# A mixture-of-experts stage: one expert group on all tokens, three groups on gathered tokens

## The reference

```python
p_group = softmax(t @ w_rg + b_rg)
g_val, g_idx = top_k(p_group, 1)
fine_sel = take_along_axis(fine, g_idx[:, :, None], axis=1)[:, 0]
e_val, e_idx = top_k(softmax(fine_sel), 2)
...
for e in range(16):
    y_e = (silu(t @ w1[e]) * (t @ w3[e])) @ w2[e]
    out = out + combine[:, e:e + 1] * y_e
```

## Time and profile before

| | |
|---|---|
| median of three runs | 2156.91 us |
| the profiled execution | 2160.48 us |
| its span (first to last instruction) | 2158.6 us |
| mean granted TensorE clock | 0.919 |
| TensorE, VectorE, ScalarE busy | 87%, 55%, 39% |
| the router's 64 matmuls | 1587.8 to 1601.6 us |
| experts, first to last matmul | 1608.3 to 2153.4 us |

### The profile page before, as it was taken

How to read it: one execution, slowest core, us unless ns; L and a number is a source line. 1 busy time by engine, 2 the same in 40 slices (tenths; PEclk the granted TensorE clock), 3 DMA queues, 4 the chain that set the end, 5 groups by cost and what they waited for, 6 DMA issues and landing times.

```text
span 2158.6 us, 28995 instructions
## 1 busy us (share of the span) xinstructions
PE 1884.3 (87%) x10182; PEld 1542.8 (71%) x10182; DVE 1194.5 (55%) x1894; ACT 844.8 (39%) x1321; POOL 16.1 (1%) x31
## 2 busy tenths in 40 slices
PE   4989887689999995996599978888779999999999
PEld 2833344568888874774489967666569999999998
DVE  3335444354444446788766665664645565555654
ACT  4122221432233234676444543442424444444432
POOL 1000000000000000000000000000000000000000
PEclk9979888879999997998889988898879999999999
DMA  7334563212333330332336633231316665656663
GB/s 279 94 125 156 201 223 122 78 43 95 98 96 97 97 97 11 87 99 77 117 118 193 186 126 98 78 98 59 91 47 185 185 194 175 194 175 193 189 182 117
DMA packets 306495, 279.37 MB, mean 129 GB/s; under 512 B 18954, under 2 KB 248828, under 8 KB 300284
## 3 DMA queue, kind: packets, MB, share of 16 engines
q1 hardware_dynamic: 304752, 269.93, 39.8%
q0 software_dynamic: 1152, 8.39, 1.0%
q10 hardware_dynamic: 524, 0.19, 0.0%
HBM read 277.40 MB, written 1.05 MB: 129 GB/s over the span
## 4 chain that ended last, share of the span: by engine, by line
PE 76%; DVE 13%; ACT 4%; DMA 4%; issue 2%; ACTq 0%; SPq 0%; DVEq 0%; POOL 0%; POOLq 0%
PE bank L366 64%; DMA ada_rows_in<-in_ada_w_dram 3%; PE bank L471 2%; PE bank L858 2%; PE bank L883 2%; PE bank L876 1%; DVE weights_lo L339 1%; PE bank L1163 1%; DVE work L549 1%; DVE x_and_ctx L552 1%; DMA work<-in_c_ctx_dram 1%; PE bank L1213 1%; DVE work L1752 1%; DVE work L1789 1%; DVE act_lo L418 1%
## 5 line engine op out<-in xcount | busy, mean ns | idle before, releaser
L339 DVE TENSOR_TENSOR weights_lo<-stage,weights_hi 128x1024 fp32r<-128x1024 f32 x428 | 516.7, 1220 | 117.2 <-ACT weights_hi L327 114.6
L366 PE MATMUL bank<-act_hi,weights_hi 128*128 128x256 f32 (+1 forms) x1744 | 534.8, 307 | 23.7 <-DVE x_and_ctx L1752 12.4
L366 PE MATMUL bank<-act_lo,weights_hi 128*128 128x256 f32 (+1 forms) x1744 | 533.7, 306 | 0.0
L366 PE MATMUL bank<-act_hi,weights_lo 128*128 128x256 f32 (+1 forms) x1744 | 533.6, 306 | 0.0
L327 ACT ACTIVATE weights_hi<-stage 128x1024 fp32r<-128x1024 f32 x428 | 439.5, 1052 | 155.5 <-PE bank L366 71.7
L366 PEld LDWEIGHTS bank<-act_hi,weights_hi 128*128 128x128 f32 x1744 | 337.8, 194 | 39.3 <-issue 18.2
L366 PEld LDWEIGHTS bank<-act_lo,weights_hi 128*128 128x128 f32 x1744 | 337.7, 194 | 14.3
L366 PEld LDWEIGHTS bank<-act_hi,weights_lo 128*128 128x128 f32 x1744 | 337.4, 193 | 13.4
L366 PE MATMUL bank<-weights_hi,ff_hi 128*128 128x512 f32 x656 | 255.7, 390 | 1.9 <-DVE ff_lo L1916 1.9
L366 PE MATMUL bank<-weights_hi,ff_lo 128*128 128x512 f32 x656 | 255.6, 390 | 0.0
L366 PE MATMUL bank<-weights_lo,ff_hi 128*128 128x512 f32 x656 | 255.4, 389 | 0.0
(11 more groups left out here) (284 smaller groups left out, 1990.2 us busy)
## 6 DMA issues: line engine op xcount, KB each, us to landing
stage<-in_w_dram SPq DMA_DIRECT2D x384, 256.0 KB, 3.3
stage<-in_mlp_w_dram SPq DMA_DIRECT2D x256, 256.0 KB, 3.0
ada_rows_in<-in_ada_w_dram SPq DMA_DIRECT2D x40, 1024.0 KB, 5.0
stage<-in_w_in_dram SPq DMA_DIRECT2D x64, 256.0 KB, 3.2
stage<-in_lru_w_in_dram SPq DMA_DIRECT2D x40, 256.0 KB, 3.5
ada_rows_in<-in_ada_w_dram POOLq DMA_DIRECT2D x8, 1024.0 KB, 13.6
stage<-in_attn_w_qkv_dram SPq DMA_DIRECT2D x24, 256.0 KB, 4.3
stage<-in_lru_w_out_dram SPq DMA_DIRECT2D x20, 256.0 KB, 3.4
```

Of the source, the lines that this page charges most:

```text
L339: dve.eng.tensor_tensor(wlo[u % NRING][:], stage[u % NSTAGE][:], whi[u % NRING][:].bitcast(F32), ALU.subtract).then_inc(sem("lo_ready"), 1)
L366: m = pe.eng.matmul(ps, l, r, start=start and j == 0, stop=stop and j == 2, skip_group_check=True)
```

## The change

- All experts of one group, the one chosen by more than 128 tokens, or else group 0, are computed on all tokens as before (e = 0 to 3 of the new loop). The other three groups are computed on blocks of 128 slots, into which the tokens of that group are gathered (e = 4 to 15).
- To do so, the router's choice of both token tiles is worked out in one pass. TensorE counts tokens by group with a triangular matrix; VectorE derives the wide group, the order of the groups (`order`, four integers) and each token's slot, and writes a 0/1 matrix `SEL` of 256 tokens by 384 slots. TensorE gathers by multiplying the normalized rows (in hi and lo parts) with `SEL`, turns `SEL` for the way back, and brings the combine weights to the slots.
- SyncE waits for `expert_order`, loads four registers from it, and addresses expert weights by register. No expert weight is loaded or split before that (`CAP`). The order of units is w1 of e, w3 of e, w2 of e - 1, and all have 512 columns. The loop over experts is unrolled.
- For a gathered expert tokens are stationary and 512 columns of weights move, so Silu and product lie token by slot; the product is turned by four transposes. The four experts of a group add up in two banks, which are split into hi and lo and scattered back by matmuls with the turned `SEL`.
- The result is stored in four transfers. The semaphores of the norms and residuals are shared between stages. Scratch for the router lies elsewhere.

```diff
+            sp.eng.wait_ge(sem("expert_order"), 1)
+            first = [sp.eng.value_load(order[0:1, g:g + 1], min_val=0, max_val=12) for g in range(4)]
+            def matrix(w, e):
+                return w[0].rearrange("e k n -> k e n")[:, ds(first[e // 4] + e % 4, 1), :].rearrange("k e n -> k (e n)")
...
+            for e in range(NEXP):
+                up_units(w1_2, e)
+                up_units(w3_2, e)
+                if e:
+                    down_units(e - 1)
+            down_units(NEXP - 1)
...
+            t.wait_ge(sem("select"), 2)
+            t.wait_ge(sem("xn_lo"), 2)
+            for d in range(KT):
+                if plan.uses[4 + d % 4]:
+                    t.wait_ge(*pe.bank_free(4 + d % 4))
+                ps = pe.take(("gather", d), 4 + d % 4)
+                for tt in TWO:
+                    for j, src in enumerate((XNH, XNL)):
+                        mm = t.matmul(ps[:, 0:384], src[:, tt, d * P:d * P + P], SEL[:, tt, :],
+                                      start=tt == 0 and j == 0, stop=tt == 1 and j == 1)
+                mm.then_inc(*pe.fill(("gather", d)))
...
+            def expert_up(e, j):
+                if e < 4:
...
+                                mm = three(pe, psum[2 * j + m // 2][:, (m % 2) * TX:(m % 2) * TX + TX],
+                                           wh[:, kk, m * P:m * P + P], wl[:, kk, m * P:m * P + P], hh_(k), hl_(k),
+                                           k == 0 and m % 2 == 0, k == KT - 1, True)
...
+                for kq in range(4):
+                    wh, wl = unit_begin(pe, (2, 512))
+                    for kk in range(2):
+                        k = 2 * kq + kk
+                        mm = three(pe, ps[:], wh[:, kk, :], wl[:, kk, :], gh[:, k, at], gl[:, k, at], k == 0,
+                                   k == KT - 1, False)
+                    unit_end(pe, mm, ("h", e, j) if kq == 3 else None)
...
+            for e in range(NEXP):          # TensorE
+                expert_up(e, 0)
+                if e > 4:
+                    expert_turn(e - 1)
+                expert_up(e, 1)
+                if ends_block(e - 2):
+                    scatter(block_of(e - 2))
+                if e:
+                    expert_down(e - 1)
...
+            for e in range(NEXP):          # ScalarE
+                if ends_block(e - 2):
+                    block_hi(block_of(e - 2))
+                expert_silu(e)
+                if e:
+                    expert_hidden_hi(e - 1)
+                    split_hi(act, 4)
+                split_hi(act, 8)
...
+            for e in range(NEXP):          # VectorE
+                if ends_block(e - 2):
+                    block_lo(block_of(e - 2))
+                if e:
+                    expert_hidden_lo(e - 1)
+                if 0 <= e - 2 < 4:
+                    expert_sum(e - 2)
+                if e:
+                    split_lo(dve, 4)
+                split_lo(dve, 4)
+                expert_product(e)
+                if ends_block(e - 2):
+                    block_sum(block_of(e - 2))
+                split_lo(dve, 4)
```

More of the change, by code:

```diff
@@ L321, in split_hi @@
                 u, per = act.unit, unit_step(act)
-                if act.i is None and u >= TOTAL[0]:
+                if act.i is None and u >= CAP.get("act", TOTAL[0] - 12 * NEXP):
                     return
@@ L680, in rnn_tile @@
             return buf[:, k // 2, (k % 2) * TX:(k % 2) * TX + TX]
[L682 to L688, removed]
         def small_loads(e):
@@ L1215, in _ @@
             mm.then_inc(*pe.fill("router"))
[L1217 to L1229, removed]
+            t.wait_ge(sem("r_group"), 1)
@@ new lines, in _ @@
+            if plan.uses[1]:
+                t.wait_ge(*pe.bank_free(1))
+            ps = pe.take("count", 1)
+            group = rt(2, 2, 4)
+            for it in range(2):
+                for jt in range(it + 1):
+                    t.matmul(ps[:, 4 * it:4 * it + 4], TRI[:, 0, jt, it * P:it * P + P], group[:, jt, :],
+                             start=jt == 0, stop=jt == it)
+            for jt in range(2):
+                mm = t.matmul(ps[:, 8:12], TRI[:, 0, 0, P:TX], group[:, jt, :], start=jt == 0, stop=jt == 1)
@@ new lines, in expert_down, with scatter @@
+                        unit_end(pe, mm, ("y", block_of(e), n) if e % 4 == 3 and fp == 1 else None)
+            def scatter(b):
+                t.wait_ge(*pe.freed(("y", b, 1)))
+                for n in range(2):
+                    for tt in TWO:
+                        bank = (3, 4, 5, 1)[2 * n + tt]
+                        if plan.uses[bank]:
+                            t.wait_ge(*pe.bank_free(bank))
+                        ps = pe.take(("sc", b, n, tt), bank)
+                        for j in range(2):
+                            mm = t.matmul(ps[:], SELT[:, b, tt * P:tt * P + P],
+                                          Yhl[:, 2 * (b % 2) + j, n * 512:n * 512 + 512], start=j == 0, stop=j == 1)
+                        mm.then_inc(*pe.fill(("sc", b, n, tt)))
@@ new lines, in _ @@
+            v.wait_ge(*dve.own())
+            v.tensor_reduce(weight, fine.rearrange("p t g k -> p t k g"), AX.X, ALU.add).then_inc(*dve.mark())
+            v.wait_ge(*dve.own())
+            v.wait_ge(*dve.filled("count"))
+            ps = plan.bank("count")
+            wide, upto, slot = rt(9, 4), rt(10, 4), rt(11, 2, 4)
+            idx, one = rt(12, 4), rt(13, 4)
+            v.tensor_scalar(wide, ps[:, 8:12], 128.5, None, ALU.is_gt).then_inc(*dve.mark())
+            v.wait_ge(*dve.own())
@@ new lines, in _ @@
+            v.wait_ge(*dve.own())
+            v.tensor_tensor(slot, slot, group, ALU.mult).then_inc(*dve.mark())
+            v.wait_ge(*dve.own())
+            v.tensor_reduce(one[:, 0:2], slot, AX.X, ALU.add).then_inc(*dve.mark())
+            v.wait_ge(*dve.own())
+            for tt in TWO:
+                v.tensor_scalar(SEL[:, tt, :], iota[:], one[:, tt:tt + 1], None, ALU.is_equal).then_inc(*dve.mark("select"))
+            first_max(o1, weight, f1, sp2)
+            v.scalar_tensor_tensor(out=weight, in0=o1, scalar=NEG, in1=weight, op0=ALU.mult, op1=ALU.add).then_inc(*dve.mark())
```

563 lines of the change are left out of this document (376 added, 187 removed).

## The result

The changed kernel takes 2043.11 us (median of four runs, 2040.79 to 2044.21) against 2157.27 for the kernel before: a ratio of 0.9467, 95% interval 0.9451 to 0.9484. It is faster by 114 us. Forecast were 1992 us and a range to 2042; the direction was right, two thirds of the gain came, and the time lies 1 us above the range. On a chip beside two of the experiments it took 2044.79 us (0.9475, 0.9455 to 0.9496).

A forecast was written before the change was run, and what follows sets the result against it. TensorE columns bound the expert stage; after the change the four-slot staging loop would bound its gathered part. 2160.48 - 545.0 + 136.2 + 225 + 15 + 4 gave 1995.7 us, as a median 1992; range 1972 to 2042 us.

The forecast's parts named there:

- What bounds the kernel now, and the price of a column: Expert stage before the change: TensorE columns are the time; 0.120 us per 256-column matmul, 0.228 per 512, 34.06 an expert.
- The loop is late next: Gathered experts: reloading four staging slots sets the pace just ahead of TensorE, 1.58 us a unit, 19.0 us an expert.
- block ends: Gathered part: at three block ends extra VectorE and ScalarE work makes the loop stand about 2.2 us each time.
- sign of being wrong: Gathered part: weight splits 1.8 us apart or more, instead of 1.58, would show slow transfers and a wrong forecast.
- rival (b): Gathered part: transfers slow under sustained demand, 1.66 to 2.21 us a unit; 2029 us at 1.85, 2003 to 2079; chance 0.25.
- the credit of six ready units: Start of the gathered part: some 6 of 144 units already lie split in the ring of eight, leaving 138 x 1.58.
- The way in: Router's result to first expert matmul: 21.7 us instead of 6.66, so +15; ends +11 and +22.
- The way out: Last expert product to the end of the span: 7.5 us instead of 5.2, in all +4; ends +2 and +7.
- What was costed at nothing: Norms and residuals: renamed and shared semaphores change counts, not waits, 0; dropping weights loaded and split ahead gives nothing.
- The rule on row length: Weight transfers: 512 B already reaches line rate, so 2 KB rows are no quicker; by it 2.21 us a unit, 2079 us.
- The 2.21 us a unit of the earlier trace: Loop with 512-byte rows, read from conversions at 1052.52 and, four units on, 1061.37; taken as the upper end, 312 us.
- (a): Gathered part: TensorE stays the bound, 214 us instead of 225, giving 1981 us; chance 0.17.

The follow-up runs named there:

- bank 4: Slot weights in bank 4 instead of bank 1, against the changed kernel with four slots: 2034.45 us (0.9434); together with six slots: 1983.06 us (0.9177).
- six slots: Six staging slots instead of four from the units of expert 4 on, against the changed kernel: 1993.20 us, ratio 0.9240.
- Copy first: Copy of the slot weights out of bank 1 put ahead of VectorE's four weight subtractions, against the changed kernel: 2038.38 us, ratio 0.9446.
- the two six-slot runs: Six staging slots instead of four against the changed kernel: 1993.20 us; the same with slot weights in bank 4 instead of bank 1: 1983.06 us.

## Why the prediction was wrong, step by step

- **What bounds the kernel now, and the price of a column: right.** The dense part runs as before: 912 matmuls of the first four experts and 24 of the fifth take 132.75 us; by the earlier trace rows that is 768 x 0.120 + 168 x 0.228 = 130.5, and the first ones run at the lower clock (0.50); where they did not (bank 4), the same matmuls took 130.42. The gathered matmuls cost what was said: where TensorE is fed (six slots), the pitch is 18.0 us with the scatters in it, against 17.4 + 0.45.
- **"The loop is late next": right, and mis-sized. This is the step that failed.** Said: "1.58 us a unit, 19.0 us an expert". Measured: 1.87 and 22.4. The loop was put together from one reload with four transfers in flight after an empty queue: 3.4 to 4.2 us from subtraction to conversion. In the steady state these are 4.6 and 5.1 us in the two rounds of the chain shown (1821.03 to 1825.64, 1828.04 to 1833.12), and the loop is 7.4 us instead of 6.3. With its block ends the forecast pitch was 19.5 us; over eleven distances the difference is 32 us. It was also named beforehand as a sign of being wrong (splits 1.8 us apart or more).
- **The reason behind it.** The rival (b), "the transfers are slow under sustained demand", had the size (1.85 us a unit), and I gave it 0.25. Its reason was half right. Landings do get longer as more transfers are in flight, but no rate caps them at the 305 to 316 GB/s that I had worked out from busy shares: the same engines move 361 GB/s with six slots.
- **Between the dense and the gathered part** 6 us were missed. TensorE waits from 1759.9 to 1766.05 while ScalarE and VectorE, in order, first do the hidden parts of the last dense expert and four additions, and only then split the next weights. The time from the first expert matmul to the last is 408.0 us, where the forecast comes to 363 (136.2 + 225 and half of the 3.1 us at the end). Of these 45 us, 32 are the loop, 6 this wait and some 2 the lower clock at the start. The other 5 may lie where the credit of six ready units (9.5 us) was taken; no run singles them out.
- **The way in: +22.3 instead of +15, the upper end given.** The steps were right or too dear: the masks are done 7.2 us after the router's result (7.5 said), the small matmuls end after 18.5 (21.7 said). What was missed is a wait that the change adds: bank 1 is handed to the slot weights, and the copy that frees it is queued behind four weight subtractions. I had named the queue behind ScalarE's splits, not that behind VectorE's. Copy first and bank 4 show it.
- **The way out: +2.2 instead of +4.** From the last expert matmul to the end of the span 7.4 us, as worked out (7.5); the four small stores land after 2.2 us, not 3.0.
- **What was costed at nothing.** In the profile after, the router's result comes 3.6 us earlier (1598.09 against 1601.68). Over the twelve profiles of changed kernels this moment lies between 1595.4 and 1608.9 us, though nothing ahead of it differs between them; the spread is there already at about 360 us. The kernel before lies inside this spread. Its cause was not tried; the 3.6 us can't be told from the spread, and as they shorten the time they are luck for the forecast, which they bring close to its range.
- **Sum.** 45.3 (first to last expert matmul) + 7.3 (way in) - 0.3 (way out, less what is in the first term) - 3.6 = 48.7 us; the span after is 48.6 us longer than forecast.
- **The rule on row length** that I weighed against the trace was nearly right, and my price for disobeying it was not. 512-byte rows cost 0.9 us an expert. The 2.21 us a unit of the earlier trace rows were misread: they are not the loop alone. Conversions from 1052.52 to 1061.37 were counted, but the last one waited for no transfer. ScalarE first did three activations of another line, and the second transfer of that unit, issued at 1055.62, landed 4.6 us later, at 1060.2 (the last line):

```profile
1059.94 1.55 ACT L1408 ACTIVATE work<-bank 128x512 f32<-128x512 f32 x3
1061.37 2.01 ACT L327 ACTIVATE weights_hi<-stage 128x1024 fp32r<-128x1024 f32 x2
...
DMA to landing us min/median/max: 4.6/4.6/4.6
```

Up to that landing it is 7.7 us for four units, 1.92 a unit, and the run with 512-byte rows has 1.94 (23.3 / 12). The Trainium skill ("DMA: Bandwidth & Descriptors", Specifications) calls 512 B enough for the line rate; this case's run gives 272 GB/s for rows of 512 bytes and 283 for 2 KB, both in the loop of four slots.
- **Two slips in the sums**, which change nothing: (a) with the shorter way in and out is 1981 - 6 = 1975, not 1974; and the part of (b) above 1.9 us a unit, called its upper third, is more than half of its width (1.66 to 2.21).

## What to carry to other kernels

When an engine gets faster, follow a buffer around its loop (freed, issued, landed, used, freed), and price it with the landing time of that many transfers in flight, not of one burst; then slots x work per slot / loop is the pace, and a few more slots can be worth a large part of the change itself: here two slots gave 50 us, the change 114. A bank or buffer that is borrowed for something small is held until the instruction that empties it comes up on its engine: look at what is queued ahead of it. Not the smallest work on the chain but the last release decides when the next stage starts.

## What the runs showed of the hardware

- The busy share of the DMA engines is no measure of what they have left: 0.88 at 283 GB/s, 0.90 at 315, 1.00 at 361, all with rows of 2 KB; 0.97 at 272 with rows of 512 bytes. The Trainium skill ("DMA: Bandwidth & Descriptors", Specifications) puts the HBM limit of a core at about 358 GB/s. The trace goes past it: 361 GB/s over 170 us in the two six-slot runs, and 383 over 14 us in one of them. Since TensorE set the pace there, no run shows where the ceiling lies.
- A transfer of 128 KB landed 2.2 us after its issue (median), one of 256 KB after 3.9, one of 512 KB after 4.7, each with four slots. The first is of a run in which TensorE set the pace (183 GB/s), the others of runs in which the loop did (283 and 282).
- TensorE kept its upper clock level nearly throughout (0.95) while it idled 67 of 230 us in waits of some 0.5 us a unit. After the single wait of 10.4 us at the start of the experts it was at the lower level (0.50), as after 6.8 us before; with bank 4, which takes that wait away, it was at the upper level from the first expert matmul on, and the dense part was 2.3 us shorter.
